# A two-block transformer kernel on one core: the mixer's level operands in one VectorE operation each, with the next tile's turned rows read between levels 2 and 3

## The chip, the core and the metric

The kernel runs on one core of a Trainium2 chip. A core has TensorE (matrix products and transposes, into PSUM), VectorE, ScalarE and GpSimd (work on 128 partitions), and SyncE, which here issues the transfers. Each engine does its own instructions in the order in which they are written; one engine waits for another by semaphores. The metric is the device time of one execution in microseconds, the median of several runs.

## The reference, cut to what matters

The reference is two layers of one block, then one of another. The change touches the mixer of the first block, above all its gated linear attention, and the order of work in that block's feed-forward stage.

```
def gla_chunked(q, k, v, log_a):
    """Causal gated linear attention. q, k, log_a: (B, S, H, dk); v: (B, S, H, dv).
    S_t = diag(alpha_t) S_{t-1} + k_t^T v_t ;  o_t = q_t S_t   (evaluated chunkwise)."""
...
        b = jnp.cumsum(gc, axis=2)
        o_inter = jnp.einsum('bhcd,bhde->bhce', qc * jnp.exp(b), state)
        diff = b[:, :, :, None, :] - b[:, :, None, :, :]
        decay = jnp.exp(jnp.where(causal[:, :, None], diff, -jnp.inf))
        attn = jnp.sum(qc[:, :, :, None, :] * kc[:, :, None, :, :] * decay, axis=-1)
        o_intra = jnp.einsum('bhij,bhje->bhie', attn, vc)
...
def first_block(...):
    for l in range(DEPTH):
        mod = (cond @ w_ada[l] + b_ada[l])[:, None, :]
        shift_a, scale_a, gate_a, shift_f, scale_f, gate_f = jnp.split(mod, N_MOD, axis=-1)
        h = rms_norm(x) * (1.0 + scale_a) + shift_a
        mix = hybrid_mixer(h, cos, sin, ...)
        x = x + gate_a * mix
        h = rms_norm(x) * (1.0 + scale_f) + shift_f
        x = x + gate_f * (jnp.square(jax.nn.relu(h @ w_mlp_up[l])) @ w_mlp_down[l])
```

The sequence has 1024 positions, the model 1024 channels; there are 4 linear-attention heads with 64 key and 128 value channels, and two layers.

## The kernel before

**Tiles.** The mixer of a layer runs over 8 tiles of 128 positions. Within a tile the linear attention is made by levels: the 128 x 128 matrix of a head splits into the diagonal and, for each of seven levels lv = 0 to 6, the blocks in which queries of the later half of a stretch of 2^(lv+1) positions meet keys of its earlier half. For a level both operands are scaled by decays relative to the middle of the stretch, so that one product serves all its blocks.

**Layout.** Four heads of 64 channels lie as two groups `g` of 128 partitions: two heads, or sides `a`, in partitions 0 to 63 and 64 to 127. `V.qk[:, 0:2]` holds the queries of both groups, `V.qk[:, 2:4]` the keys. A product over 128 partitions would mix the two sides. So `V.sided[:, lv, a, g]` holds queries of side `a` in their 64 partitions and zeros in the others; the product of the keys with it gives each head its own scores. GpSimd clears `V.sided` once a layer (L820, 128 x 1792), and VectorE writes only the 64 rows of each side.

**VectorE in a tile** (`dve_mixer`): the gate's logarithm and its running sum, the exponents of the decays (L1242 to L1248), normalised latents (L1253, L1254), query times key for the diagonal (L1258), then `dve_operands` for the levels 0 to 6. That is, but for level 0, the keys times decays (L1201, 128 x 128), and for every level the queries times decays, once for each side (L1207, 64 x 128, twice). Then `dve_turned_x` (L1180, four operations of 128 x 128) reads four of the eight 128 x 128 pieces of the next tile's transposed input rows out of PSUM, scales and shifts them and puts them in `V.hT`: these are "the turned rows". ScalarE does the other four (L1048). Both must wait until the value product of this tile (signal "v") has read the old `V.hT`. Behind the turned rows VectorE has L1266 (keys for the state), L1267, L1269, the query sums (L1271, L1272), the key sums (L1274), the means, the diagonal (L1283), the scores of levels 0 and 1 put into `V.attn` (L1192), the norms and the rotated rows (L1287 to L1306), levels 2 to 6 (L1192) and the state.

**TensorE in a tile** (`pe_mixer`): latents, the turn of the next tile's rows, the value product, the query products from the latents (`q_up`), then a wait for the next tile's turned rows of both engines, the key-value products (`kv_up`), the next tile's gate input, the diagonal, levels 0 and 1, the next tile's queries and keys (`pe_qk`), levels 2 to 4, the turns of the rotated rows (`turn_qpe`, `turn_kpe`, `turn_kd`), level 5 and so on. Its waits are semaphores, put where the code says.

**ScalarE in a tile** (`act_mixer`): among others it copies the value product (L1120), does its turned rows (L1048), copies the query products (L1127) and the key-value products (L1133, L1136), squares the keys (L1140), which needs the query sums since both use one scratch place, and in `act_qk` copies the next tile's queries (L1066, times 1/8) and keys (L1067) out of PSUM bank 1. The turns of the rotated keys go to that bank too.

**Feed-forward stage.** The up product runs over 16 chunks n; a chunk has seven products p of sums and differences of quarters (a Strassen-like scheme), each of 12 matmuls for a split into a high and a low part, in the order 2, 5, 6, 3, 7, (1 of the next chunk), 4. Products 6 and 3 wait for VectorE's first sum of the chunk (`c11`, L2435), product 7 for the middle sum (`mid`, L2445). Besides, in layer 0 the modulation of layer 1 is made in 16 units, one a chunk: SyncE loads the weights of unit u (L479, L480) once VectorE is done with unit u - 1, VectorE sums over them (`dve_ada_unit`, L492, eight operations), and TensorE adds over partitions (`pe_ada_unit`, one column). VectorE does unit 1 at the very end of chunk 1 and unit n within chunk n afterwards.

Of the kernel before, what the change touches and what calls it, by code (L numbers as in the profile page):

```python
# [5 lines left out]
ALU = mybir.AluOpType  # L6
# [5 lines left out]
P = 128  # L12
# [12 lines left out]
EPS = 1e-6  # L25
TAU = 16.0
LEVELS = P.bit_length() - 1
MASKED = -1e30
TWO_PI = 2 * np.pi
MAGIC = 1.5 * 2.0 ** 23  # L30
# [558 lines left out]
def mixer_views(k):  # L589
    V = k.mix = Views()  # L590
    ring = Area(k.weights.rearrange("p a b -> p (a b)"))
    V.kT, V.val = ring.take(MH, S), ring.take(NT, MH * MV)
    A = Area(k.arena, 8192)
    V.w_qk, V.w_am, V.w_v, V.w_o = A.take(KC, 512), A.take(KC, GR + 448), A.take(KC, 512), A.take(KC, 512)
    V.rt = A.take(2, MH + 1, HALF_ROPE)
    V.first_q = V.rt.rearrange("p a h f -> p (a h f)")[:, 0:P]
    A = Area(k.arena, 0)
    V.decays = A.take(P + (LEVELS - 1) * 2 * P)
    V.decay0, V.decay = shaped(V.decays[:, 0:P], (2, P // 2)), shaped(V.decays[:, P:], (LEVELS - 1, 2, P))
    V.sided, V.prod = A.take(LEVELS, 2, 2, P // 2), A.take(2, P)  # L600
    A.at = 3 * LEVELS * 2 * P
    V.attn, V.qh, V.kn = A.take(GH, P), A.take(MH * (NOPE + ROPE)), A.take(MH * NOPE)
    V.pe_in, V.pe_rot, V.eb = A.take(MH + 1, ROPE), A.take(MH + 1, ROPE), A.take(2, P)
    A = Area(k.arena, 24576)
    V.xt, V.xn = A.take(D), A.take(D)
    V.go, V.vt, V.o, V.o_sq = (A.take(GH * DV) for _ in range(4))
    V.hT, V.wkv_up = A.take(KC, P), A.take(MH * (NOPE + MV))
    V.qk, V.ga, V.z, V.la, V.b = A.take(4, P), A.take(P), A.take(2, P), A.take(2, P), A.take(2, P)
    V.ebl, V.m_q = A.take(2, P), A.take(QR + KVR)
    V.wq_up, V.w_gate, V.qe = A.take(2, MH * (NOPE + ROPE)), A.take(GH * DK), A.take(2, P)  # L610
    V.kd, V.kdn, V.state, V.mT, V.q_out = A.take(2, P), A.take(2, P), A.take(2, 2 * DV), A.take(3, P), A.take(MH, P)
    A = Area(k.arena, 36864)
    V.kpeT, V.qpe_out = A.take(S), A.take(MH, P)
    k.kT, k.kpeT, k.val = V.kT, V.kpeT, V.val
    V.tmp = k.scratch[:, 0:MH * (NOPE + ROPE)]
    g = k.small
    V.qa_g, V.kva_g, V.qn_g, V.kn_g, V.bg, V.out_g = g[:, 0:2], g[:, 2:3], g[:, 3:4], g[:, 4:5], g[:, 5:7], g[:, 8:8 + DV]
    V.pe_g = g[:, 256:256 + (MH + 1) * ROPE].rearrange("p (h r) -> p h r", r=ROPE)
    V.q3, V.t3, V.kn3, V.o3, V.go3 = (x.rearrange("p (h n) -> p h n", h=MH) for x in (V.qh, V.tmp, V.kn, V.o, V.go))
# [184 lines left out]
def pool_mixer(k, l):  # L804
# [3 lines left out]
    pool_rsqrt(k, st[:, 1:2], st[:, 0:1], D).then_inc(*out.up("x", l, 0))  # L808
    before_mixer(k, E, l)
    gp.memset(V.state, 0.0).then_inc(*out.up("zero", l))  # L810
    for t in range(NT):
        if t + 1 < NT:
            E.wait_ge(S_.mix_act.at("sq_x", l, t + 1))
# [1 line left out]
        E.wait_ge(S_.mix_act.at("m_read", l, t))  # L815
        pool_rsqrt(k, st[:, 4:5], st[:, 4:5], QR).then_inc(*E.up())
        pool_rsqrt(k, st[:, 5:6], st[:, 5:6], KVR).then_inc(*out.up("m", l, t))
        if t == 0:
            before_levels(k, E, l)
            gp.memset(V.sided, 0.0).then_inc(*out.up("sided", l))  # L820
        E.wait_ge(S_.mix_dve.at("means", l, t))
        gp.tensor_tensor(st[:, 8:21], st[:, 8:21], k.minus_half(13), ALU.pow).then_inc(*out.up("heads", l, t))
        if t == NT - 1:
# [236 lines left out]
def act_qk(k, l, t):  # L1060
    S_, E, V = k.S, k.act, k.mix
    s, out = k.nc.scalar, S_.mix_act
    E.wait_ge(S_.mix_pe.at("qk", l, t))
    if t > 0:
        E.wait_ge(S_.mix_dve.at("qe", l, t - 1), S_.mix_pe.at("level", l, t - 1, 0))
    s.activation(V.qk[:, 0:2, :], k.ps[1][:, 0:256].rearrange("p (a b) -> p a b", a=2), ACT.Copy, scale=DK ** -0.5).then_inc(*out.up("q_raw", l, t))  # L1066
    s.activation(V.qk[:, 2:4, :], k.ps[1][:, 256:512].rearrange("p (a b) -> p a b", a=2), ACT.Copy).then_inc(*out.up("qk", l, t))  # L1067


# [125 lines left out]
def dve_operands(k, l, t, lv):  # L1195

    S_, V, v = k.S, k.mix, k.nc.vector
    q, kk = V.qk[:, 0:2, :], V.qk[:, 2:4, :]
    if lv > 0:
        even = half_blocks(V.decay[:, lv - 1], lv, 0)  # L1200
        v.tensor_tensor(even, half_blocks(kk, lv, 0), even, ALU.mult)  # L1201
        late = half_blocks(V.decay[:, lv - 1], lv, 1)
    else:
        late = odd_blocks(V.decay0, 0)
    for a in range(2):
        r = slice(64 * a, 64 * a + 64)
        i = v.tensor_tensor(odd_blocks(V.sided[r, lv, a], lv), half_blocks(q, lv, 1)[r], late[r], ALU.mult)  # L1207
    i.then_inc(*S_.mix_dve.up("operands", l, t, lv))


def dve_mixer(k, l):
# [8 lines left out]
    for t in range(NT):  # L1220
# [35 lines left out]
        if t > 0:  # L1256
            E.wait_ge(pe.at("diag", l, t - 1))
        v.tensor_tensor(V.prod, V.qk[:, 0:2, :], V.qk[:, 2:4, :], ALU.mult).then_inc(*out.up("prod", l, t))  # L1258
        if t == 0:
            E.wait_ge(pool.at("sided", l))  # L1260
        for lv in range(LEVELS):
            dve_operands(k, l, t, lv)
        if t + 1 < NT:
            dve_turned_x(k, l, t + 1)
        E.wait_ge(act.at("ebl", l, t))
        v.tensor_tensor(V.kd, V.qk[:, 2:4, :], V.ebl, ALU.mult).then_inc(*out.up("kd", l, t))  # L1266
        v.tensor_tensor(V.qe, V.qk[:, 0:2, :], V.eb, ALU.mult).then_inc(*out.up("qe", l, t))  # L1267
# [1470 lines left out]
def pe_ff(k, l):  # L2738
    for n in range(FFC):
        if n > 1:  # L2740
            pe_up(k, l, n, 2)
        for p in (5, 6, 3, 7):
            pe_up(k, l, n, p)
            if p == 3 and n == 1 and l + 1 < DEPTH:
                pe_ada_unit(k, l + 1, 0)
        if 0 < n < FFC - 1:
            pe_up(k, l, n + 1, 1)
        pe_up(k, l, n, 4)
        if l + 1 < DEPTH and n > 0:
            pe_ada_unit(k, l + 1, n)  # L2750
    for q in range(TURNS):
        pe_down(k, l, q)
# [2161 lines left out]
```

## Time and profile before

| | us |
|---|---|
| median of 3 runs | 3485.04 |
| lowest and highest run | 3484.25, 3485.05 |
| the profiled execution | 3482.96 |
| its span, first to last instruction | 3481.7 |

The profile is of one execution; its own time lies 2.1 us below the median. Times in its rows are counted from the span's start. A row of a timeline gives the start, the time to the end, the engine, the line, the operation and, in brackets, how long the engine stood idle before it and whose end let it go on. PE is TensorE, DVE VectorE, ACT ScalarE, SPq the queue in which SyncE issues transfers. "xN" are N instructions of one form in a row, with the time from the first start to the last end. A VectorE instruction's time overlaps that of the next: what one costs is the distance from start to start.

### The profile page before, as it was taken

The page shows a single profiled execution, that of the slowest core. Times are in us where ns is not written, and L with a number is a line of the kernel's source. Part 1 is how long each engine was busy: PE and PEld are TensorE (multiplying, and loading weights), DVE is VectorE, ACT ScalarE, POOL GpSimd, SP SyncE. Part 2 cuts the span into 40 slices and gives each one's busy share as a digit, 9 for nine tenths or more (in the row PEclk, how much of TensorE's full clock was granted, in tenths as well). Part 3 has the DMA queues.
Part 4 walks back from the last instruction along what each step waited for, and adds up shares of the span by engine and source line. Part 5 has one row for each costly group of instructions (what it writes and reads, how often), then busy time and mean ns, then how long its engine had stood idle before and what let it go on. Part 6 is the DMA issues. An engine that isn't in the chain of part 4 may idle for free. (4 is left out here: it accounts for less than half of the span.)

```text
span 3481.7 us, 41880 instructions
## 1 busy us (share of the span) xinstructions
PE 3351.2 (96%) x16163; PEld 2267.4 (65%) x16163; DVE 1991.0 (57%) x3850; ACT 1279.0 (37%) x2233; POOL 439.8 (13%) x561
## 2 busy tenths in 40 slices
PE   7999899999999999998999999999999997999998
PEld 4666567688888876665676887888775683333333
DVE  3666785877757666667847666576664743000002
ACT  2444333455544344443334555443430621111101
POOL 1111110000000001111100000000110002444443
PEclk9999999999999999999999999999999998999999
DMA  6000372355575560003623444754600317887634
GB/s 235 28 28 22 126 250 98 127 176 175 186 258 193 193 226 28 28 22 125 244 93 108 154 149 170 254 194 169 208 15 2 128 67 292 280 307 248 208 97 121
DMA packets 270290, 525.17 MB, mean 151 GB/s; under 512 B 46256, under 2 KB 117624, under 8 KB 263948
## 3 DMA queue, kind: packets, MB, share of 16 engines
q1 hardware_dynamic: 238716, 398.56, 32.7%
q0 software_dynamic: 29920, 123.28, 10.7%
q8 instruction: 128, 2.10, 0.2%
q10 hardware_dynamic: 1456, 0.66, 0.1%
q14 instruction: 70, 0.57, 0.1%
HBM read 615.18 MB, written 114.82 MB: 210 GB/s over the span
## 5 line engine op out<-in xcount | busy, mean ns | idle before, releaser
L225 PE MATMUL psum<-arena_r,arena_r 128*128 128x512 f32 (+1 forms) x4916 | 1166.1, 389 | 7.8 <-DVE arena L2455 3.2
L225 PEld LDWEIGHTS psum<-arena_r,arena_r 128*128 128x128 f32 x4916 | 921.4, 188 | 199.1 <-issue 11.6
L225 PE MATMUL psum<-arena 128*128 128x128 f32 (+9 forms) x3338 | 780.4, 394 | 27.8 <-DVE arena L1180 19.8
L225 PEld LDWEIGHTS psum<-arena 128*128 128x128 f32 (+1 forms) x3338 | 472.8, 192 | 285.1 <-issue 211.2
L4555 PE MATMUL psum<-arena 128*64 128x512 f32 x1536 | 342.1, 598 | 6.9 <-DMA arena<-in_expert_w_gate,be_i 5.6
L2380 ACT ACTIVATE arena_r<-arena 128x1024 fp32r<-128x1024 f32 x192 | 192.4, 1052 | 327.3 <-PE psum L225 304.2
L2595 DVE TENSOR_TENSOR arena_r<-arena,arena_r 128x1024 fp32r<-128x1024 f32 x192 | 226.0, 1221 | 132.3 <-ACT arena_r L2380 132.3
L268 POOL TENSOR_SCALAR stat<-stat 128x1 f32<-128x1 f32 (+1 forms) x120 | 39.0, 325 | 1961.8 <-ACT arena L1032 671.8
L4687 DVE TENSOR_TENSOR arena<-arena,psum 128x512 f32<-128x512 f32 x24 | 16.5, 688 | 428.2 <-PE psum L4555 428.2
L233 PEld LDWEIGHTS psum<-const,arena 128*128 128x128 f32 (+1 forms) x1439 | 169.8, 153 | 128.2 <-issue 86.3
L4555 PEld LDWEIGHTS psum<-arena 128*64 128x64 f32 x1536 | 109.4, 138 | 215.9 <-issue 212.2
L233 PE MATMUL psum<-const,arena 128*128 128x128 f32 (+1 forms) x1439 | 208.3, 283 | 28.1 <-DVE arena L1309 7.4
L225 PE MATMUL psum<-arena_r,weight_ring_r 128*128 128x512 f32 (+1 forms) x816 | 189.3, 389 | 1.3 <-DVE arena_r L3118 1.3
L4555 PE MATMUL psum<-weight_ring,arena 128*64 128x512 f32 x768 | 171.7, 600 | 2.1 <-DMA weight_ring<-in_expert_w_up,be_i 2.1
L225 PE MATMUL psum<-weight_ring,arena 128*128 128x128 f32 (+3 forms) x820 | 166.7, 349 | 3.9 <-DVE gate L459 1.8
L225 PEld LDWEIGHTS psum<-arena_r,weight_ring_r 128*128 128x128 f32 x816 | 149.4, 188 | 31.1 <-DVE arena_r L3118 1.6
L225 PE MATMUL psum<-arena,weight_ring 128*128 128x512 f32 x352 | 155.4, 598 | 3.2 <-DVE arena L2455 1.7
L225 PEld LDWEIGHTS psum<-weight_ring,arena 128*128 128x128 f32 x820 | 108.9, 193 | 37.4 <-issue 35.9
L4645 ACT ACTIVATE arena<-psum 128x512 f32<-128x512 f32 x24 | 14.3, 598 | 320.9 <-PE psum L4555 320.9
L225 PE MATMUL psum<-weight_ring_r,arena_r 128*128 128x512 f32 x358 | 128.6, 403 | 0.0
L225 PEld LDWEIGHTS psum<-arena,weight_ring 128*128 128x128 f32 x352 | 66.5, 192 | 84.0 <-issue 81.9
L4555 PEld LDWEIGHTS psum<-weight_ring,arena 128*64 128x64 f32 x768 | 53.5, 138 | 102.8 <-issue 97.8
(471 smaller groups left out, 3952.7 us busy)
## 6 DMA issues: line engine op xcount, KB each, us to landing
tmp_hidden<-arena SPq DMA_DIRECT2D x224, 256.0 KB, 2.0
arena<-tmp_hidden SPq DMA_DIRECT2D x112, 512.0 KB, 4.5
arena<-in_w_mlp_down SPq DMA_DIRECT2D x96, 512.0 KB, 6.2
arena<-in_w_ada SPq DMA_DIRECT2D x36, 1024.0 KB, 6.7
weight_ring<-in_w_mlp_up SPq DMA_DIRECT2D x32, 1024.0 KB, 5.7
tmp_x_res<-arena SPq DMA_DIRECT2D x32, 512.0 KB, 5.1
arena<-tmp_x_res SPq DMA_DIRECT2D x24, 512.0 KB, 8.4
arena<-in_w_in SPq DMA_DIRECT2D x4, 2048.0 KB, 15.1
```

What stands on the lines that cost most here:

```text
L225: i = self.nc.tensor.matmul(out, lhs, rhs, start=start and n == 0, stop=stop and n == len(pairs) - 1, skip_group_check=read_between)
L233: i = self.nc.tensor.transpose(out, in_, self.ident(in_.shape[0]))
L268: k.nc.gpsimd.tensor_scalar(out, total, 1.0 / width, EPS, ALU.mult, ALU.add).then_inc(*G.up())
L2380: k.nc.scalar.activation(V.raw_hi[part][q % 2], src, ACT.Copy).then_inc(*S_.down_act.up(l, q, part))
L2595: k.nc.vector.tensor_tensor(V.raw_lo[part][slot], src, V.raw_hi[part][q % 2].bitcast(F32), ALU.subtract).then_inc(*S_.down_dve.up("low", l ...
L4555: i = k.nc.tensor.matmul(bank[at(c, BLOCK), :], left[:, b, at(c, BLOCK)], w[c][:, b, at(a, 512)], start=b == 0, stop=b == n - 1)
L4645: k.nc.scalar.activation(V.sg[s % 2], k.ps[3], ACT.Silu).then_inc(*S_.ex_act.up("silu", s))
L4687: v.tensor_tensor(V.su, V.sg[s % 2], k.ps[2], ALU.mult).then_inc(*S_.ex_dve.up("su", s))
```

## The change

It has three parts. First, `V.q_sided`, new, lies in a place of `k.gate` that is free during the mixer; GpSimd clears it once a layer, and in each tile ScalarE copies the queries of either side into its 64 partitions, so that the queries are laid out by sides, with zeros. VectorE then makes the queries of a level, for both sides and all 128 partitions, zeros included, in one operation of 128 x 256 (L1213 of the kernel after). `V.sided` need not be cleared. Second, the turned rows of the next tile are read between levels 2 and 3 and no longer behind level 6. Third, TensorE takes unit 1 of the modulation within chunk 2, before product 7, and no longer at the end of chunk 1.

```diff
+TURNED_BEFORE = 3
...
+    V.q_sided = shaped(k.gate[:, 1, 512:1024], (2, 2, P))
...
     gp.memset(V.state, 0.0).then_inc(*out.up("zero", l))
+    gp.memset(V.q_sided, 0.0).then_inc(*out.up("sided", l))
...
-        if t == 0:
-            before_levels(k, E, l)
-            gp.memset(V.sided, 0.0).then_inc(*out.up("sided", l))
...
     s.activation(V.qk[:, 0:2, :], k.ps[1][:, 0:256].rearrange("p (a b) -> p a b", a=2), ACT.Copy, scale=DK ** -0.5).then_inc(*out.up("q_raw", l, t))
+    if t == 0:
+        E.wait_ge(S_.mix_pool.at("sided", l))
+    for a in range(2):
+        r = slice(64 * a, 64 * a + 64)
+        s.activation(V.q_sided[r, a], k.ps[1][r, 0:256].rearrange("p (a b) -> p a b", a=2), ACT.Copy, scale=DK ** -0.5)
     s.activation(V.qk[:, 2:4, :], k.ps[1][:, 256:512].rearrange("p (a b) -> p a b", a=2), ACT.Copy).then_inc(*out.up("qk", l, t))
...
 def dve_operands(k, l, t, lv):
...
-    for a in range(2):
-        r = slice(64 * a, 64 * a + 64)
-        i = v.tensor_tensor(odd_blocks(V.sided[r, lv, a], lv), half_blocks(q, lv, 1)[r], late[r], ALU.mult)
+    half = 2 ** lv
+    into = V.sided[:, lv].rearrange("p a g (n h) -> p a (g n) h", h=half)
+    both = V.q_sided.rearrange("p a g (n b h) -> p a (g n) b h", b=2, h=half)[:, :, :, 1, :]
+    i = v.tensor_tensor(into, both, spread(late.unsqueeze(1), P, 2, P // half, half), ALU.mult)
...
-        if t == 0:
-            E.wait_ge(pool.at("sided", l))
         for lv in range(LEVELS):
+            if lv == TURNED_BEFORE and t + 1 < NT:
+                dve_turned_x(k, l, t + 1)
             dve_operands(k, l, t, lv)
-        if t + 1 < NT:
-            dve_turned_x(k, l, t + 1)
...
-            if p == 3 and n == 1 and l + 1 < DEPTH:
-                pe_ada_unit(k, l + 1, 0)
+            if p == 3 and n in (1, 2) and l + 1 < DEPTH:
+                pe_ada_unit(k, l + 1, n - 1)
         if 0 < n < FFC - 1:
             pe_up(k, l, n + 1, 1)
         pe_up(k, l, n, 4)
-        if l + 1 < DEPTH and n > 0:
+        if l + 1 < DEPTH and n > 1:
             pe_ada_unit(k, l + 1, n)
```

Three places show how the instructions now stand. The first is VectorE in a tile that has a next one, from the operation ahead of level 0; before, L1207 is a level's queries (two of 64 rows), L1201 its keys, L1180 the turned rows:

```order
L1258 TENSOR_TENSOR arena<-arena 128x256
L1207 TENSOR_TENSOR arena<-arena 64x128 x2
L1201 TENSOR_TENSOR arena<-arena 128x64x2
...
L1201 TENSOR_TENSOR arena<-arena 128x2x64
L1207 TENSOR_TENSOR arena<-arena 64x128 x2
L1180 TENSOR_SCALAR arena<-psum,mod 128x128 x4
L1266 TENSOR_TENSOR arena<-arena 128x256
```

The same place in the kernel after, where L1213 is a level's queries, L1206 its keys, L1185 the turned rows and L1270 the old L1266:

```order
L1264 TENSOR_TENSOR arena<-arena 128x256
L1213 TENSOR_TENSOR arena<-gate,arena 128x256
L1206 TENSOR_TENSOR arena<-arena 128x64x2
L1213 TENSOR_TENSOR arena<-gate,arena 128x256
L1206 TENSOR_TENSOR arena<-arena 128x32x4
L1213 TENSOR_TENSOR arena<-gate,arena 128x256
L1185 TENSOR_SCALAR arena<-psum,mod 128x128 x4
L1206 TENSOR_TENSOR arena<-arena 128x16x8
L1213 TENSOR_TENSOR arena<-gate,arena 128x256
...
L1270 TENSOR_TENSOR arena<-arena 128x256
```

The turned rows stand behind three levels and ahead of four, and a level's queries are one operation.

The second place is ScalarE at the key squares of a tile and the copies for the next, before:

```order
L1140 ACTIVATE scratch<-arena 128x512
L1141 ACTIVATE scratch,stat<-arena 128x64
L1066 ACTIVATE arena<-psum 128x256
L1067 ACTIVATE arena<-psum 128x256
L1149 ACTIVATE arena<-psum 64x512
```

and after:

```order
L1145 ACTIVATE scratch<-arena 128x512
L1146 ACTIVATE scratch,stat<-arena 128x64
L1066 ACTIVATE arena<-psum 128x256
L1071 ACTIVATE gate<-psum 64x256 x2
L1072 ACTIVATE arena<-psum 128x256
L1154 ACTIVATE arena<-psum 64x512
```

Two copies of 64 rows stand between the queries' copy and the keys'.

The third is TensorE at the end of chunk 1 in layer 0; the names are the high and low parts of weights and inputs, "const,arena 128x1" is a unit of the modulation. Before:

```order
L225 MATMUL psum<-weight_ring_r_53,scratch_r_72 128x512
L225 MATMUL psum<-arena,weight_ring 128x512 x4
L225 MATMUL psum<-const,arena 128x1
L225 MATMUL psum<-weight_ring_r_53,arena_r_73 128x512
L225 MATMUL psum<-arena_r_55,arena_r_73 128x512
```

and after, there and before product 7 of chunk 2:

```order
L226 MATMUL psum<-weight_ring_r_53,scratch_r_72 128x512
L226 MATMUL psum<-arena,weight_ring 128x512 x4
L226 MATMUL psum<-weight_ring_r_53,arena_r_73 128x512
...
L226 MATMUL psum<-arena_r_65,arena_r_69 128x512
L226 MATMUL psum<-const,arena 128x1
L226 MATMUL psum<-arena_r_63,arena_r_77 128x512
```

The unit moved behind products 2, 5, 6 and 3 of chunk 2.

## Rows read from the trace of the kernel before

**Rows 1.** The page, busy time, share of the span and instructions of an engine:
```profile
PE 3351.2 (96%) x16163; PEld 2267.4 (65%) x16163; DVE 1991.0 (57%) x3850; ACT 1279.0 (37%) x2233; POOL 439.8 (13%) x561
```
**Rows 2.** Line L1180: who waited for it (us, times):
```profile
  PE psum L225: 19.8, 14
```
**Rows 3.** Timeline of TensorE in tile 1 of layer 0, 113 to 136 us:
```profile
114.72 4.46 PE L225 MATMUL psum<-arena 128*128 128x512 f32 x12
120.46 1.98 PE L225 MATMUL psum<-arena 128*128 128x512 f32 x4 [1.28 <-DVE arena L1180]
...
133.32 0.93 PE L233 MATMUL psum<-const,arena 128*64 128x128 f32 x7
```
**Rows 4.** Timeline of TensorE in tile 0 of layer 0:
```profile
69.22 0.55 PE L233 MATMUL psum<-const,arena 128*128 128x128 f32 x3 [2.30 <-DVE arena L1254]
```
**Rows 5.** Timeline of VectorE in tile 1, 113 to 121 us:
```profile
113.52 0.58 DVE L1207 TENSOR_TENSOR arena<-arena 64x128 f32<-64x128 f32 x2
114.13 0.29 DVE L1201 TENSOR_TENSOR arena<-arena 128x128 f32<-128x128 f32 x1
114.33 0.58 DVE L1207 TENSOR_TENSOR arena<-arena 64x128 f32<-64x128 f32 x2
...
119.04 1.37 DVE L1180 TENSOR_SCALAR arena<-psum,mod 128x128 f32<-128x128 f32 x4
120.32 0.42 DVE L1266 TENSOR_TENSOR arena<-arena 128x256 f32<-128x256 f32 x1
120.65 0.42 DVE L1267 TENSOR_TENSOR arena<-arena 128x256 f32<-128x256 f32 x1
```
**Rows 6.** Timeline of ScalarE in tile 1, 116 to 133 us:
```profile
116.63 0.60 ACT L1120 ACTIVATE arena<-psum 128x512 f32<-128x512 f32 x1 [0.83 <-PE psum L225]
117.13 1.50 ACT L1048 ACTIVATE arena<-psum,mod 128x128 f32<-128x128 f32 x4
...
123.35 0.62 ACT L1140 ACTIVATE scratch<-arena 128x512 f32<-128x512 f32 x1
...
131.74 0.39 ACT L1066 ACTIVATE arena<-psum 128x256 f32<-128x256 f32 x1 [7.53 <-PE psum L225]
132.02 0.38 ACT L1067 ACTIVATE arena<-psum 128x256 f32<-128x256 f32 x1
```
**Rows 7.** Timeline of VectorE in tile 1, query sums and rotated rows:
```profile
122.18 0.41 DVE L1272 TENSOR_REDUCE stat<-scratch 128x4 f32<-128x256 f32 x1
...
131.54 0.32 DVE L1306 TENSOR_TENSOR arena<-arena 128x160 f32<-128x160 f32 x1
```
**Rows 8.** Timeline of ScalarE in the last tile of layer 0:
```profile
379.75 0.63 ACT L1140 ACTIVATE scratch<-arena 128x512 f32<-128x512 f32 x1 [0.60 <-DVE stat L1272]
```
**Rows 9.** Timeline of VectorE and TensorE in chunks 1 and 2, layer 0:
```profile
681.16 3.06 DVE L492 SCALAR_TENSOR_TENSOR arena<-arena,cond 128x128 f32<-128x128 f32 x8
684.27 0.59 PE L225 MATMUL psum<-const,arena 128*128 128x1 f32 x2 [6.06 <-DVE arena L492]
684.30 0.69 DVE L2408 TENSOR_TENSOR scratch_r<-weight_ring,scratch_r 128x512 fp32r<-128x512 f32 x1
...
689.07 11.04 PE L225 MATMUL psum<-arena_r,arena_r 128*128 128x512 f32 x48
...
691.08 3.06 DVE L492 SCALAR_TENSOR_TENSOR arena<-arena,cond 128x128 f32<-128x128 f32 x8
...
694.71 0.69 DVE L2445 TENSOR_TENSOR arena<-arena,psum 128x512 f32<-128x512 f32 x1
```
**Rows 10.** Stretches: length; busy PE, PEld, DVE, ACT, POOL; granted clock; DMA:
```profile
684.70:689.05 4.35, 4.35 (x13) 3.46 (x14) 0.29 (x1) 0.00 (x0) 0.00 (x0) 0.63 0.70 222
...
69.22:71.00 1.78, 1.77 (x6) 1.03 (x7) 0.81 (x3) 1.78 (x4) 0.00 (x0) 0.76 0.00 0
```
**Rows 11.** Timeline of SyncE's queue at the load of unit 2:
```profile
684.54 0.38 SPq L480 DMA_DIRECT2D arena<-in_w_ada  x1
```
**Rows 12.** The page, transfers: count, KB each, median us from issue to landing:
```profile
arena<-tmp_hidden SPq DMA_DIRECT2D x112, 512.0 KB, 4.5
```

More of the change, by code:

```diff
@@ L1197, in dve_operands @@
     S_, V, v = k.S, k.mix, k.nc.vector
-    q, kk = V.qk[:, 0:2, :], V.qk[:, 2:4, :]
+    kk = V.qk[:, 2:4, :]
     if lv > 0:
```

## The prediction

> **What bounds the kernel now.** The page comes first: TensorE is busy for 96% of the span [rows 1]. So the time is TensorE's own work plus its waits, and an edit pays only as far as it shortens one of its waits. Next I asked for each line that the change moves who waited for it. VectorE's turned rows (L1180) are what TensorE waited for 14 times, 19.8 us in all [rows 2]: once in each tile that has a next one, seven in each of two layers. Last I read one such tile engine by engine. TensorE ends the query products at 119.18 (114.72 + 4.46), stands for 1.28 us and starts the key-value products at 120.46 [rows 3]; over the fourteen a wait is 1.4 us in the mean. Before the turned rows VectorE makes the operands of seven levels, one after the other, from 113.52 to 119.04 [rows 5]. ScalarE's half of the turned rows is done at 118.63 (117.13 + 1.50) [rows 6], before TensorE wants it. So this wait belongs to VectorE's order of work.
>
> **Part 1: one operation for a level's queries.** Before, a level takes two operations of 64 rows x 128, the second starting at partition 64. The pair holds the engine 0.61 us (113.52 to 114.13), the key operation after it 0.20 (114.13 to 114.33) [rows 5]. After, it is one of 128 x 256 with both operands in memory. The nearest row is L1266, the same operation and size: the next starts 0.33 us later (120.32 to 120.65) [rows 5]. I take 0.33. A level saves 0.28, seven save 1.9 us of VectorE per tile. What the trace does not show is this operation with the decays repeated over the sides. Bounds: from 0.20, the row of half the size, to 0.61, the old pair.
>
> The pair is slower than two single operations, 0.61 against 2 x 0.20. The Trainium skill, VectorE: DVE Perf Modes, section "Two Vector instructions with no wait between them", says why: an operation whose input or output starts in another quadrant of partitions than the last one's is held until all before it have finished. By that rule the new row of operations, all starting at partition 0, is not held, and the trace agrees with it in the 0.20 and the 0.33; were they held all the same, each at its full 0.42 us, levels 3 to 6 would end 0.7 later and the slack in (b) below would fall from 1.1 to 0.4, which would speak for the first rival.
>
> **Part 2: turned rows between levels 2 and 3.** VectorE starts level 0 at 113.52. Levels 0 to 2 take 3 x 0.33 + 2 x 0.20 = 1.4, to 114.9. The turned rows must then wait for the value product, which still reads the old ones; ScalarE starts its copy of that product, released by TensorE, at 116.63 [rows 6]. So VectorE stands 1.7 us and does the four turned rows from 116.65, in 1.28 (119.04 to 120.32) [rows 5], to 117.95. They are ready 1.2 us before TensorE asks at 119.18, ScalarE's half 0.55 before. The whole wait goes: 14 waits, **19.8 us**. Queued behind the new wait are levels 3 to 6: 4 x 0.53 = 2.1, to 120.1. The next operation (L1266) stood at 120.32 before, so all that follows on VectorE keeps its place or gains 0.2.
>
> What is late next? TensorE comes 1.28 earlier to everything. (a) Squares of the keys: ScalarE starts them at 123.35 [rows 6]; they need the query sums from VectorE, which end at 122.59 [rows 7] and shift by only 0.2, to 122.4, so the squares come 0.95 earlier, not 1.28. (b) From there the rotated rows follow, ended at 131.86 [rows 7], new about 130.9. TensorE turns them at 133.32 [rows 3], new 132.04: slack 1.1. (c) The operands of levels 3 to 6 are due only after the next tile's query products, which ScalarE takes at 131.74 [rows 6]. Nothing replaces the wait in my count.
>
> **Part 3: ScalarE lays out the queries.** Two copies of 64 x 256 more per tile. The row L1066, 128 x 256 from the same bank, holds ScalarE 0.28 us (131.74 to 132.02) [rows 6]; two cost 0.56, between nothing and 0.78 at their full 0.39. They delay the end of the keys' copy, before at 132.40, now 132.40 - 1.28 + 0.56 = 131.7. TensorE wants that bank for its turns after 132.04, and ScalarE itself waited 7.53 us before these copies [rows 6]. Cost nothing; without this cover it would be 0.56 x 14 = 8 us.
>
> **Part 4: clears.** GpSimd no longer clears the seven levels' operands once a layer and clears the queries' place instead, before the first tile; ScalarE's wait for it falls long after. Nothing either way.
>
> **Part 5: last tile of each layer.** It has no turned rows, so all 1.9 us of VectorE reach the query sums. ScalarE waited 0.60 us for those [rows 8], two such rows, one a layer, and TensorE then waits for VectorE's chain behind them. No more than 0.60 can come of it, since ScalarE itself is free only then; I take 0.5 each, **1.0 us**.
>
> **Part 6: the unit in the feed-forward stage.** TensorE no longer waits for unit 1 at the end of chunk 1, where it stood 6.06 us until 684.27 [rows 9]; it takes it after four products of chunk 2. After the stand the granted clock was 0.63 of full in the stretch of that chunk's first product [rows 10], which took 4.35 us against 11.04 / 4 = 2.76, start to start 2.72, for each of the next four (48 operations) [rows 9]. Now: the first product starts at 678.2 (684.27 - 6.06), ends at 680.9, the second at 683.7. The third needs VectorE's first sum of chunk 2. That stands behind unit 1 (681.16 + 3.06) and the low part at 684.30 [rows 9], so it is done at 684.91 + 0.69 = 685.6: TensorE waits 1.9. Third and fourth end at 691.1. The fifth needs the middle sum, behind unit 2. Unit 2's weights are asked for at 684.54 as before [rows 11], since this hangs on unit 1; another load of 512 KB lands in 4.5 us [rows 12], so at 689.0. Unit 2 and one more sum take 3.63 (691.08 to 694.71) and the middle sum 0.69 [rows 9]: 693.4. Before, the fifth product began at 697.2 (689.07 + 3 x 2.72). Gain **3.8 us**. Bounds: weights there only at 691.08, where VectorE began before: fifth product at 695.4, gain 1.8. Weights there at once: 691.2, gain 6.0. A fallen clock for one stretch like that of [rows 10] takes 1.6 off again: the new waits are 1.9 and 2.3, and a wait of 2.30 [rows 4] was followed by a stretch at 0.76 [rows 10]. So 0.2 to 6.0.
>
> **The sum.** 19.8 + 1.0 + 3.8 = 24.6 us off the profiled execution's 3482.96 gives 3458.4. That execution lies 2.1 below the median of the runs, 3485.04; the forecast for the median is 3485.04 - 24.6 = **3460.4**, with a range of its own from 3456 to 3465.
>
> **Rivals.**
> *The wait moves (0.13).* VectorE now stands 1.7 us within its row, and the rotated rows' slack (1.1) is used up by a late sum or by ScalarE's order; TensorE gets half of each wait back. For it: the key squares gain less than TensorE does. Against: the slack is worked out from a tile that the 13 others resemble. 9.9 + 1 + 3.8 = 14.7: 3470.3.
> *Nothing is gained (0.06).* The turned rows are not the last thing awaited: ScalarE's half ends later, too, or the feed-forward stage and the tiles give it back at other waits. Against: 118.63 is before 119.18. About 3483.
> *Slower by a slow operation (0.05).* The decays are repeated over the sides and the queries read with gaps. The chain to the rotated rows has 2.2 us before it reaches TensorE's old time: 0.76 from the query sums to the key squares (122.59 to 123.35) and 1.46 from the rotated rows to the turns (131.86 to 133.32). L1266 may thus start at 122.5; from 117.95 that leaves 4.6 for four levels: it decides at 0.95 us per operation. At 1.2, levels 0 to 2 end at 117.5, the turned rows at 118.8, level 6 at 124.4, 4.1 late, the turns 1.9 after their old time: 14 x 1.9 - 4.8 = +22: 3507. Against: L1266 shows 0.33 and even the old pair 0.61 [rows 5].
> *The feed-forward part yields nothing (0.10)*, late weights and a fallen clock: 3464, inside the own range.
> The forecast itself has 0.66.
>
> **How the numbers follow.** About 0.2% (7 us) is what a measurement of this kernel can tell from no change. Forecast, moved wait and empty feed-forward part lie below 3478: faster 0.89. Nothing gained, 0.06, is same. Slower 0.05. The range holds 8 in 10: from 3455, should the feed-forward part give its 6.0 and the half clock spare a stretch, to 3471, which takes in the moved wait.
>
> **What would show it.** Right: no wait of TensorE before the key-value products; VectorE idle about 1.7 us before the turned rows, released by TensorE; tiles shorter by 1.3 to 1.4 us; the new operation starting 0.33 us before the next; two waits near 683.7 and 691 less the shift, in place of 6.06. Wrong: a new wait of TensorE at the turns of the rotated rows or for the keys' copy; tiles as long as before; an operation of 0.9 us; the middle sum not before 695.

## The result and the profile after

The changed kernel takes 3454.99 us, median of 4 runs (3454.14 to 3456.33), beside 3485.05 for the kernel before (4 runs, 3484.25 to 3488.08): ratio 0.9913, interval 0.9895 to 0.993, so 30.1 us faster. The forecast was 24.6 us, 3460.4; the measured time lies 5.4 us below the forecast and 0.01 us below the low end of the wide range (3455 to 3471). Put on a chip again later, the same kernel took 3453.18 us beside 3485.21. The profiled execution of after has a span of 3452.6, 29.1 shorter than before.

The page, in the same columns as [rows 1]: VectorE lost 112 instructions and 26 us, ScalarE gained 32 and 10 us.

```profile
span 3452.6 us, 41796 instructions
PE 3348.0 (97%) x16163; PEld 2270.9 (66%) x16163; DVE 1965.1 (57%) x3738; ACT 1288.9 (37%) x2265; POOL 443.0 (13%) x561
```

Who waited for the turned rows is the first thing to ask. The view of that line (L1185 after) lists under the last heading nobody, where [rows 2] had 19.8 us in 14 waits. Instead VectorE itself now waits, 13 times for TensorE's value product:

```profile
its engine sat idle before it (us, times) until:
  PE psum L226: 20.7, 13
  PE psum L234: 3.6, 1
who waited for it (us, times):
```

TensorE in tile 1 of layer 0, to be laid beside [rows 3] (start, duration, engine, line and operation):

```profile
114.17 6.18 PE L226 MATMUL psum<-arena 128*128 128x512 f32 x16
120.28 0.64 PE L850 MATMUL psum<-arena 128*32 128x128 f32 x16
...
131.23 0.93 PE L234 MATMUL psum<-const,arena 128*64 128x128 f32 x7
```

The row of 12 (the last four value products and the eight query products) and the 4 key-value products have run together into one row of 16. From 119 us on the view shows the four alone: they start at 118.47 and take 1.88 us, `x4`. The turns of the rotated rows at 131.23 have no wait in front.

VectorE in the same tile, beside [rows 5]:

```profile
113.39 0.42 DVE L1213 TENSOR_TENSOR arena<-gate,arena 128x256 f32<-128x256 f32 x1
113.73 0.29 DVE L1206 TENSOR_TENSOR arena<-arena 128x128 f32<-128x128 f32 x1
113.93 0.42 DVE L1213 TENSOR_TENSOR arena<-gate,arena 128x256 f32<-128x256 f32 x1
...
116.16 1.37 DVE L1185 TENSOR_SCALAR arena<-psum,mod 128x128 f32<-128x128 f32 x4 [1.27 <-PE psum L226]
...
119.58 0.43 DVE L1270 TENSOR_TENSOR arena<-arena 128x256 f32<-128x256 f32 x1
...
130.16 0.32 DVE L1310 TENSOR_TENSOR arena<-arena 128x160 f32<-128x160 f32 x1
```

The new operation holds the engine 0.34 us (113.39 to 113.73) where the old pair held it 0.61.

**Tiles with late latents.** The 14 waits of before are not alike. Beside the first tiles of the two layers (1.70 and 0.72), seven are 1.26 to 1.28 us long and five are 1.69 to 1.71. In those five tiles VectorE's normalised latents waited 1.43 us for GpSimd, where it is 0.19 in tile 1, and the whole row behind them is 0.4 later, TensorE's wait with it. Tile 3 of before:

```profile
198.92 0.48 DVE L1253 TENSOR_SCALAR arena<-psum,stat 128x256 f32<-128x256 f32 x1 [1.43 <-POOL stat L270]
206.86 1.98 PE L225 MATMUL psum<-arena 128*128 128x512 f32 x4 [1.70 <-DVE arena L1180]
```

Which tiles these are differs from one execution to the next. The kernel with the unit alone (below) has the mixer of before, none of these five tiles is late in its profile, and the line of its turned rows says:

```profile
  PE psum L225: 17.7, 14
```

So 2.1 of the 19.8 us belong to that one execution. Tile 1 of after, shown above, is late, too; tile 2 is not, and VectorE stands longer there ahead of the turned rows:

```profile
157.61 1.37 DVE L1185 TENSOR_SCALAR arena<-psum,mod 128x128 f32<-128x128 f32 x4 [1.70 <-PE psum L226]
```

In after a tile takes 41.44 us, late or not.

**Where the 29.0 us lie.** The same instruction of TensorE is looked up in both traces; start before less start after, taken at the borders of the stages, gives what each stage gained in the two profiled executions:

| stage | gain, us | forecast |
|---|---|---|
| start to first tile | -1.49 | 0 |
| the 14 waits before the key-value products | 23.40 | 19.8 |
| last tile of each layer | 0.75 + 0.29 | 1.0 |
| feed-forward stage of layer 0 | 3.98 | 3.8 |
| near 1747 us | 1.38 | 0 |
| the rest | 0.7 | 0 |

The 14 waits alone gave 3.6 us more than their recorded idle time. The first row and the last two are most likely no work of the change: in the profile of the kernel with the unit alone, whose start is that of before, the first row is -2.7. TensorE's clock was at half (1.2 GHz) in other stretches. Before it stood at 0.79 of full in the stretch 1744 to 1752, with a wait of 0.74 us on ScalarE in it; the same work in after, with the same wait of 0.74, ran at 1.00 (the column behind the last bracket of the busy times is the granted clock):

```profile
1744.00:1752.00 8.00, 7.26 (x19) 3.53 (x20) 0.00 (x0) 7.38 (x9) 0.00 (x0) 0.79 0.62 206
```
```profile
1717.10:1725.10 8.00, 7.24 (x23) 3.68 (x24) 0.00 (x0) 7.31 (x9) 0.00 (x0) 1.00 0.58 205
```

### The profile page after: what moved, and what is told of

Its sections match the earlier page's. It is cut to its first block and busy times, and to the rows that moved or that the text cites. A ratio compares the mean times of both kernels' runs of the same rounds, so it can differ in the third digit from the quotient of the medians.

```text
span 3452.6 us, 41796 instructions
## 1 busy us (share of the span) xinstructions
PE 3348.0 (97%) x16163; PEld 2270.9 (66%) x16163; DVE 1965.1 (57%) x3738; ACT 1288.9 (37%) x2265; POOL 443.0 (13%) x561
## 3 DMA queue, kind: packets, MB, share of 16 engines
q0 software_dynamic: 29920, 123.28, 10.8%
```

## The experiments

The theory is the account of the prediction, with the sizes that the profile of after put in its place; against it stand, run by run, the rivals that each expectation names. The first three kernels take the parts of the change one by one, the fourth goes on where the third leaves off, and the others measure the slack and the price of a wait.

### The order alone

```diff
         for lv in range(LEVELS):
+            if lv == 3 and t + 1 < NT:
+                dve_turned_x(k, l, t + 1)
             dve_operands(k, l, t, lv)
-        if t + 1 < NT:
-            dve_turned_x(k, l, t + 1)
```

> The kernel before with one edit: the turned rows are read between levels 2 and 3; a level still takes two operations of 64 rows, and the unit stays where it was. Theory A (a wait of TensorE costs 0.27 us more than its recorded idle time, since the next product would have started while the last one still ran, and the first product after a wait is slower): the wait before the key-value products is gone, and each tile gains up to 1.55 us. But levels 3 to 6 end at 117.95 + 4 x 0.81 = 121.2, 0.9 later than before, so the query sums end at 123.5 and the rotated rows at 132.0, where TensorE comes at 131.8: a wait of about 0.2 us recorded at their turns, 0.4 in cost, so 1.1 us a tile, 16 us in all: 3469 (3463 to 3473). Theory B (the extra gain in the measured kernel comes from the new operation, which relieves TensorE or its memory): at most 1.28 us minus 0.2 a tile: 3470 to 3472, with TensorE's own products slower than in the changed kernel. The start-to-start times around the key-value products tell them apart: A says 0.32 us between the last query product and the first key-value product, as in the changed kernel.

Measured: 3469.47 us (5 runs), ratio 0.9959 [0.9945, 0.9974], before beside it 3483.1 (14 runs). TensorE in tile 1:

```profile
114.37 6.18 PE L225 MATMUL psum<-arena 128*128 128x512 f32 x16
120.48 0.64 PE L850 MATMUL psum<-arena 128*32 128x128 f32 x16
...
131.86 0.95 PE L233 MATMUL psum<-const,arena 128*64 128x128 f32 x7 [0.27 <-DVE arena L1306]
```

The old wait is gone from the row of 16, and a new one of 0.27 us stands at the turns of the rotated rows: the rival "the wait moves", in small. VectorE still has the old pairs, so its four last levels take 0.82 us each and the rest of its row comes late. The same point (L850) comes again in the next tile at 162.38, so a tile takes 41.90 us; before it is 42.98 (120.46 to 163.44), in after 41.44 (120.28 to 161.72). The row of 16 takes 6.18 us here as in after, with the old operations on VectorE, so theory B, that the new operation relieves TensorE, falls.

### The operation alone

The changed kernel with the turned rows behind level 6 again and unit 1 again at the end of chunk 1.

```diff
         for lv in range(LEVELS):
-            if lv == TURNED_BEFORE and t + 1 < NT:
-                dve_turned_x(k, l, t + 1)
             dve_operands(k, l, t, lv)
+        if t + 1 < NT:
+            dve_turned_x(k, l, t + 1)
```

> The changed kernel with the turned rows back behind level 6 and the unit where it was: only ScalarE's layout and the one operation a level are left. VectorE reaches the turned rows at 113.4 + 7 x 0.34 + 6 x 0.20 = 117.0 and ends them at 118.2 to 118.3, TensorE asks at 118.5 in the frame of the changed kernel. Theory A: the wait goes in about half of the tiles and is below 0.3 recorded in those where the latents come 0.4 us late; gain about 21 us in the mixers plus 1 in the last tiles: 3463 (3460 to 3466). So the order alone and the operation alone would each do most of the work, and they don't add. The rival, that the reordering is what closes the wait: 3475 or more, with recorded waits of about 0.7 us.

Measured: 3455.92 us (4 runs), ratio 0.9917 [0.99, 0.9934]; 7 us better than expected and outside the range. TensorE and VectorE in tile 1:

```profile
113.00 6.18 PE L226 MATMUL psum<-arena 128*128 128x512 f32 x16
119.11 0.64 PE L850 MATMUL psum<-arena 128*32 128x128 f32 x16
...
130.05 0.93 PE L234 MATMUL psum<-const,arena 128*64 128x128 f32 x7
```
```profile
111.79 0.43 DVE L1213 TENSOR_TENSOR arena<-gate,arena 128x256 f32<-128x256 f32 x1
...
115.36 1.36 DVE L1185 TENSOR_SCALAR arena<-psum,mod 128x128 f32<-128x128 f32 x4
```

The turned rows end at 116.63 (start of the next operation), and the key-value products follow the query products without a wait in tiles 1 to 6. In tile 0 a wait of 0.55 us stays. A tile is again 41.44 (119.11 to 160.55), as in after. The expectation that about half of the waits would stay falls: the operation alone saves 1.9 us of VectorE, more than a steady wait costs (1.5), and in this execution the order would add nothing to it but the rest in tile 0. But none of the tiles 1 to 7 of either layer has late latents here. The turned rows end 0.39 us ahead of the load of the key-value weights (117.02), and late latents would take up those 0.39; whether a wait comes back in such a tile is not shown. The parts are not additive: order alone 13.6 us, operation alone 27.2, both and the unit 30.

### The unit alone

```diff
-            if p == 3 and n == 1 and l + 1 < DEPTH:
-                pe_ada_unit(k, l + 1, 0)
+            if p == 3 and n in (1, 2) and l + 1 < DEPTH:
+                pe_ada_unit(k, l + 1, n - 1)
...
-        if l + 1 < DEPTH and n > 0:
+        if l + 1 < DEPTH and n > 1:
             pe_ada_unit(k, l + 1, n)
```

> The kernel before with only the unit moved behind four products of chunk 2. The profile of the changed kernel gained 4.0 us between chunk 1 and the end of chunk 2, as forecast (3.8). Expected: 3481.1 (3480 to 3483), two waits of 1.9 and 1.6 us in place of 6.06, and no fall of the granted clock there. Rival: the gain there came with the shifted phase of the mixer's times, and alone the clock falls in the second wait: 3482.5 to 3484.

Measured: 3477.8 us (10 runs, 3471.67 to 3482.43), ratio 0.9986 [0.9976, 0.9995], so 5.3 us faster: 3.3 better than the expected 3481.1 and outside the range. In the profile the stage gave 4.0 us, with the waits

```profile
688.09 5.72 PE L225 MATMUL psum<-arena_r,arena_r 128*128 128x512 f32 x24 [2.09 <-DVE arena L2435]
...
695.46 3.00 PE L225 MATMUL psum<-arena_r,arena_r 128*128 128x512 f32 x12 [1.54 <-ACT arena_r L2229]
```

in place of the 6.06 of [rows 9]. The profiled execution ended 8.6 us before that of the old kernel: beside the 4.0 of the stage, 2.1 are the waits in the mixer (17.7 for 19.8), which no edit touched. Ten runs of this one kernel spread over 10.8 us, 14 of before over 10.9: that is the scatter in which any forecast of this kernel stands.

### The two waits that the unit left

If these two waits come from VectorE's order (unit 1 ahead of the first sum, unit 2 ahead of the middle sum), moving the units behind those sums must take both.

```diff
+    late = units and n == 2
+    if late:
+        dve_up_first_sum(k, l, n)
+        dve_ada_unit(k, l + 1, n - 1)
...
-    if n > 1:
+    if n > 1 and not late:
         dve_up_first_sum(k, l, n)
...
-    if units and n > 1:
+    if units and n > 2:
...
     dve_up_fourth(k, l, n)
+    if late:
+        dve_ada_unit(k, l + 1, n)
...
-        if units:
-            dve_ada_unit(k, l + 1, n)
```

> The changed kernel with VectorE's order of chunk 2 in the feed-forward stage changed: the first sum of chunk 2 directly behind chunk 1, unit 1 behind it and no longer ahead of it, unit 2 behind the fourth sum of chunk 2. Both waits that are left there (1.95 us for the first sum, 1.63 for the middle sum) should go, since TensorE's fifth product then needs a sum that is ready at about 688 in the old frame, and unit 2 has the slack of VectorE behind it: 1.95 + 1.63 + 2 x 0.27 = 4.1 us less than the changed kernel: 3450.9 (3449 to 3453). Rival: VectorE gets late for the fourth sum and the units' loads come late in chunk 3, the waits move there: 3454 to 3456.

Measured: 3448.55 us (4 runs, 3442.36 to 3452.56), ratio 0.9902 [0.9886, 0.9919]. The time is 0.45 us below the expected range. The stage gained 7.96 us on before, 4.0 more than in after, as expected. TensorE there, and VectorE's first sum and unit 1:

```profile
666.27 8.34 PE L226 MATMUL psum<-arena_r,arena_r 128*128 128x512 f32 x36
674.44 0.28 PE L226 MATMUL psum<-const,arena 128*128 128x1 f32 x2
674.58 2.99 PE L226 MATMUL psum<-arena_r,arena_r 128*128 128x512 f32 x12
```
```profile
666.60 0.68 DVE L2439 TENSOR_TENSOR arena<-arena,psum 128x512 f32<-128x512 f32 x1
667.20 3.05 DVE L493 SCALAR_TENSOR_TENSOR arena<-arena,cond 128x128 f32<-128x128 f32 x8
```

No wait is left in chunk 2. By the medians this kernel is 34.6 us faster than before on the same chip, where after is 30.1 and 32.0 faster in its two series. That is 2.5 to 4.5 more. The intervals of the ratios overlap, so it is the 4.0 of the stage, and not the medians, that shows the gain.

### How much slack the changed kernel has

Each of the levels 3 to 6 makes its queries twice; the second result goes to a place that nobody reads.

```diff
     i.then_inc(*S_.mix_dve.up("operands", l, t, lv))
+    if lv >= TURNED_BEFORE:
+        again = k.gate[:, 0, at(lv - TURNED_BEFORE, 256)].rearrange("p (a n h) -> p a n h", a=2, h=half)
+        v.tensor_tensor(again, both, spread(late.unsqueeze(1), P, 2, P // half, half), ALU.mult)
```

> The changed kernel with each query operation of levels 3 to 6 made a second time, into a place that nothing reads: four operations more on VectorE behind the turned rows, 4 x 0.33 = 1.33 us a tile. This measures the slack of the forecast and the point from which a slow operation would cost. In the changed kernel the rotated rows end at 130.48 and TensorE turns them at 131.23: slack 0.75. ScalarE's key squares wait for the query sums already (0.57 us), so the 1.33 us go through in full: the rotated rows come 0.58 after TensorE. Expected: a recorded wait of 0.4 to 0.6 us at the turns of the rotated rows, 0.6 to 0.85 us more a tile start to start, 14 tiles: plus 8 to 12 us on the changed kernel, 3463 to 3467. Rival (the sums are not what the rotated rows hang on, the slack is larger): no wait, 3455.

Measured: 3462.41 us, one run, 0.6 below the expected range. TensorE:

```profile
118.56 0.65 PE L850 MATMUL psum<-arena 128*32 128x128 f32 x16
...
130.15 0.95 PE L234 MATMUL psum<-const,arena 128*64 128x128 f32 x7 [0.48 <-DVE arena L1313]
```

A tile takes 42.11 us (118.56 to 160.67), 0.67 more than in after, for four operations of 0.34 (1.34 us of VectorE). So 0.67 of the 1.34 was covered: after's slack of about 0.75 at the rotated rows (130.48 to 131.23) is real. The rival "slower by a slow operation" had its mechanism right: operations of 0.68 instead of 0.34 are enough for a new wait at the turns. It costs 0.67 of the 1.54 that a tile gained, so the sign stays; operations slow enough to turn it were not tried.

### What a wait costs: a shorter one and a longer one

The order kernel with the turned rows before level 6 instead of level 3, and the kernel before with one more pair of operations at level 6, which writes to a place that nobody reads:

```diff
+            if lv == 6 and t + 1 < NT:
+                dve_turned_x(k, l, t + 1)
             dve_operands(k, l, t, lv)
-        if t + 1 < NT:
-            dve_turned_x(k, l, t + 1)
```

> The kernel before with the turned rows between levels 5 and 6, old operations: VectorE ends the turned rows one level, 0.81 us, earlier. Recorded wait before the key-value products: 1.28 - 0.81 = 0.47 us. If a wait costs its recorded time plus a constant 0.27, a tile shortens by 0.81 us; if the true cost is 1.21 times the recorded time, by 0.98 us. 13 to 14 us over both layers: 3470 to 3473.

```diff
+    if lv == LEVELS - 1:
+        more = k.gate[:, 0, 0:P].rearrange("p (g n h) -> p (g n) h", g=2, h=P // 2)
+        for a in range(2):
+            r = slice(64 * a, 64 * a + 64)
+            v.tensor_tensor(more[r], half_blocks(q, lv, 1)[r], late[r], ALU.mult)
```

> The kernel before with one more pair of 64-row query operations (0.61 us) ahead of the turned rows, into a place that nothing reads. Recorded wait 1.28 + 0.61 = 1.89 us. With a constant 0.27 beside it a tile lengthens by 0.61 us, 14 x 0.61 = 8.5 us: 3492 to 3494. With 1.21 times the recorded wait by 0.74 us, 3494 to 3496. If the clock falls in the longer wait, more, and the granted clock of the stretches behind it shows that.

Measured, one run each: 3469.64 us, 0.4 below the expected range, and 3499.79 us. The key-value products of tile 1 and of the next in the first:

```profile
120.92 1.98 PE L225 MATMUL psum<-arena 128*128 128x512 f32 x4 [0.45 <-DVE arena L1180]
```
```profile
163.09 1.98 PE L225 MATMUL psum<-arena 128*128 128x512 f32 x4 [0.46 <-DVE arena L1180]
```

and in the second, with the tile after that:

```profile
125.62 1.99 PE L225 MATMUL psum<-arena 128*128 128x512 f32 x4 [1.87 <-DVE arena L1180]
```
```profile
169.20 1.99 PE L225 MATMUL psum<-arena 128*128 128x512 f32 x4 [1.87 <-DVE arena L1180]
```
```profile
212.79 3.39 PE L225 MATMUL psum<-arena 128*128 128x512 f32 x4 [1.87 <-DVE arena L1180]
```

With 41.44 us as the tile without a wait, each kernel's tile gives the price of its recorded wait:

| kernel | place | recorded | tile | price | price less recorded |
|---|---|---|---|---|---|
| turned rows before level 6 | key-value products | 0.46 | 42.17 | 0.73 | 0.27 |
| before | key-value products | 1.27 | 42.98 | 1.54 | 0.27 |
| one pair more | key-value products | 1.87 | 43.58 | 2.14 | 0.27 |
| order alone | turns | 0.27 | 41.90 | 0.46 | 0.19 |
| levels doubled | turns | 0.48 | 42.11 | 0.67 | 0.19 |

The surplus does not grow with the wait: it is a constant of the place. A price of 1.21 times the recorded time, the other reading, would have shortened the tile by 0.98 us and lengthened it by 0.74; measured are 0.81 and 0.60. At the key-value products the surplus can be split from two rows. The row of 12 started at 114.72 and its record ends 4.46 later [rows 3]; in after the key-value products start 4.30 after that row's start (114.17 to 118.47). So 0.16 us of the next product's time lie within the record of the last one, and are lost unseen when it must wait. And four key-value products took 1.98 us after a wait, 1.88 without. 0.16 + 0.10 = 0.26.

The rows of TensorE's weight loads (PEld) show what is lost. Before, then after:

```profile
120.46 0.30 PEld L225 LDWEIGHTS psum<-arena 128*128 128x128 f32 x2 [1.90 <-DVE arena L1180]
```
```profile
118.20 0.46 PEld L226 LDWEIGHTS psum<-arena 128*128 128x128 f32 x2 [0.18 <-DVE arena L1213]
```

In after the key-value weights are loaded from 118.20, while the last query product runs, 0.27 us ahead of their product at 118.47. Before, the load waits for VectorE, too, and starts with the product at 120.46. The surplus is this head start of 0.27 us.

The row at 212.79 shows what made the last kernel cost more than the table says (3499.8, expected 3492 to 3496): the same four products took 3.39 us. TensorE's granted clock there, a tile with the full clock ahead of it:

```profile
124.00:128.30 4.30, 2.68 (x22) 1.25 (x22) 3.74 (x10) 2.44 (x7) 0.00 (x0) 1.00 0.00 0
212.70:217.00 4.30, 4.21 (x21) 1.63 (x21) 2.22 (x6) 1.32 (x4) 0.00 (x0) 0.60 0.00 0
301.50:305.80 4.30, 4.21 (x21) 1.58 (x21) 2.22 (x6) 1.32 (x4) 0.00 (x0) 0.60 0.00 0
```

The clock fell to half behind waits of 1.87 us in some tiles, about every second one. A fall cost about 1.6 us: the two tiles from 171.12 to 259.92 (L850) take 88.80 us, two of 43.58 would take 87.16. In the kernel before the same places are at 1.00, also behind the wait of 1.70 us at 206.86:

```profile
207.50:211.80 4.30, 4.30 (x42) 3.10 (x41) 2.62 (x9) 2.38 (x8) 0.00 (x0) 1.00 0.00 0
```

### The changed kernel again

Unchanged.

> The changed kernel once more, unchanged, to see how much of its time hangs on the places where the granted clock falls. Its profile had half clock for 10 us in the first 60 us, and none near 1747 and 686 us, where the profile of the kernel before had it. If these places differ from one execution to the next, its time lies between 3450 and 3460 and the difference of 29.0 us between the two first profiles is up to 4 us chance; the mixers' tiles, counted start to start, must repeat within 0.1 us.

Measured: 3453.18 us (4 runs, 3448.95 to 3455.15), ratio 0.9909 [0.9893, 0.9926]. The steady tiles repeat to 0.02 us. The feed-forward stage does not: here the clock fell to half at about 684 us, in the first profile of after it did not, and 1.7 us of the stage's 3.98 were given back. The half clock near 1747 is missing here, too. So the length of the changed kernel's steady tile is the change's own. The table's 23.4 us hold for the before of that one execution, with its five late tiles; against tiles that are all on time they would be 2.1 less. The rows of a microsecond or two elsewhere are those of one execution, too.

## Why the prediction was right, and where it was wrong

**The step that failed** is the term of 19.8 us: "The whole wait goes: 14 waits, 19.8 us" took the recorded idle time for the price of the wait. The mechanism, that the whole wait goes and nothing takes its place, was right, the size was off: the 14 waits measured 23.4 us. In the steady tiles the surplus is 0.27 each, in the first tile of a layer 0.23 and 0.13, in all 3.6 us. Put into the sum it gives 19.8 + 3.6 + 1.0 + 3.8 = 28.2, or 3456.8 for the median, within 2 us of the result. The 19.8 was itself the sum of one execution; the same mixer in another recorded 17.7. What is left is inside the scatter: the two profiles differ by 28.8 in the execution's time and the medians by 30.1, with half clock in other places each time.

**The range** was too narrow for the same reason: its low end came from the feed-forward part alone, and gave no room for an error in the largest term nor for the scatter of about 5 us to either side that the runs of one kernel show. By its own terms it would have been 3456.6 (3485.04 - 19.8 - 1.0 - 6.0 - 1.6), not 3455.

**Part 1** held: 0.34 us from start to start for 0.33 forecast, well inside 0.20 to 0.61. By the rule of the Trainium skill (VectorE: DVE Perf Modes, "Two Vector instructions with no wait between them") operations that all start in the same quadrant are not held; the row 113.39, 113.73, 113.93 agrees with it.

**Part 2** held in its result: no wait before the key-value products, nothing in its place. VectorE stood 1.70 us in tile 2, as forecast, and 1.27 in tile 1, whose latents were late: it began level 0 only 0.78 us ahead of TensorE's row of 16 (113.39 against 114.17), 1.20 ahead of the row of 12 before. This cost nothing. One size was off: the slack at the rotated rows was 0.75 instead of 1.1. Counted from the start of that row of TensorE, the rotated rows ended at 16.31 (forecast 130.9 - 114.72 = 16.2) and TensorE was there at 17.06 (forecast 17.3): the surplus of the wait again, which brings TensorE earlier to everything behind it.

What the prediction did not see is that it did not need the order. It worked out 1.9 us saved on VectorE per tile and stood beside it a wait of 1.28; even with the surplus, 1.9 exceeds 1.54. The second kernel shows it. The claim that the change's second part removes the waits is thus not shown; it removes them when alone, and beside the first part adds only tile 0, and perhaps the tiles with late latents, where before lost 1.97 (1.70 + 0.27) and which the second kernel's profile does not have.

**Part 3** held on the path, not in size. ScalarE's copies:

```profile
129.64 0.38 ACT L1066 ACTIVATE arena<-psum 128x256 f32<-128x256 f32 x1 [6.81 <-PE psum L226]
129.92 0.76 ACT L1071 ACTIVATE gate<-psum 64x256 f32<-64x256 f32 x2
130.69 0.38 ACT L1072 ACTIVATE arena<-psum 128x256 f32<-128x256 f32 x1
```

The two hold the engine 0.77 us (129.92 to 130.69), at the upper bound of 0.78, where 0.56 was taken. ScalarE still waited 6.81 us ahead of them, and no wait of TensorE points to it.

**Part 4** nothing, as forecast. **Part 5**: 0.75 and 0.29 in the two last tiles, 1.04 for 1.0, in part by luck. TensorE's wait for VectorE there fell from 2.50 to 1.94 and 1.95 us, but the gain across it is only 0.36 and 0.37; the other 0.39 and -0.08 arose beyond it, in and near stretches at half clock.

**Part 6** was the longest working and came out within 0.2, with luck in the clock: in the second execution the same stage gave 2.3. The stage of after, beside [rows 9]:

```profile
674.93 5.69 PE L226 MATMUL psum<-arena_r,arena_r 128*128 128x512 f32 x24 [1.95 <-DVE arena L2439]
680.46 0.28 PE L226 MATMUL psum<-const,arena 128*128 128x1 f32 x2
682.37 2.98 PE L226 MATMUL psum<-arena_r,arena_r 128*128 128x512 f32 x12 [1.63 <-ACT arena_r L2233]
```
```profile
673.81 0.38 SPq L481 DMA_DIRECT2D arena<-in_w_ada  x1
...
677.96 3.06 DVE L493 SCALAR_TENSOR_TENSOR arena<-arena,cond 128x128 f32<-128x128 f32 x8 [1.98 <-DMA arena<-in_w_ada]
```

The first wait is 1.95 (forecast 1.9). The second is 1.63 (forecast 2.3): unit 2's weights landed 4.15 us after their issue, not 4.5, and TensorE was ready for the fifth product at 691.6 and not 691.1 (682.37 - 1.63 + 10.87). The row also names a term that the prediction left out: the last to come was ScalarE's high part (L2233) of that product's weight sum, made from another sum of VectorE behind unit 2. It ended 0.07 us after the middle sum (682.29 and 682.22), so it cost next to nothing. The fifth product starts, with the 10.87 us that all stood earlier by then, at 693.24; forecast 693.4. Whether the clock falls behind these waits was put as a bound of 1.6; in the second execution it did, and cost 1.7.

**The rivals.** "The wait moves" is what the order alone does (0.27 at the turns, 0.46 in price), and the wide operation is what keeps it from the changed kernel. "Nothing is gained" and "slower" did not come.

## What to carry to other kernels

The idle time that a profile shows ahead of a matmul is less than the wait costs: here 0.19 to 0.27 us less, a constant for each place, so many short waits are worth visibly more than their sum (14 waits of 1.4 us: 18% more). Where two edits attack one wait, work out for each alone whether it closes it; if one does, the other pays only where it is not enough. And where a wait goes because an instruction is taken later, look at what else the producing engine does ahead of the next sums: putting the units behind them gave the second half of that gain.

## What the runs showed of the hardware

- A wait ahead of float32 products of 512 columns cost its recorded idle plus 0.27 us: 0.16 that the next product would have overlapped, and 0.10 by which the four products after it took longer (1.98 against 1.88). Without the wait the weights were loaded 0.27 us ahead of their product (118.20, 118.47), under the product before; behind the wait load and product start together (120.46). At the turns by 128 columns the surplus is 0.19.
- TensorE's clock fell to half (1.2 GHz) behind waits of 1.87 us, one a tile of 43.6 us, in about every second tile; with waits of 1.26 to 1.71 us in tiles of 43.0 and 43.4 us it stayed at 2.4 GHz. Why some tiles and not others is open.
- Outside the tiles, where the half clock falls differs from one execution of the same kernel to the next (at 684 us in one profile of after, not in the other). Runs of one kernel spread over 2 to 11 us, and the mean granted clock goes with them: of the ten runs with the unit alone the fastest (3471.67 us) has 0.989, the slowest (3482.43) 0.986. The late latents make another part of the difference between executions, 2.1 us in the two compared above.
- Two ScalarE copies of 64 x 256 from PSUM, at partitions 0 and 64, took 0.77 us start to start, nearly their full 0.38 each, where one of 128 x 256 holds the engine 0.28 (129.64 to 129.92). Whether the change of partitions holds them, as it holds VectorE's pairs, was not tried.
